# First attention of a two-layer kernel: keys on the partitions, one head with 512 queries as the unit

## The reference

```python
q = (rms_norm(x_q, q_norm_g) @ w_uq).reshape(B, S, 4, 192)      # 128 plain + 64 rotary features
kv = (rms_norm(x_kv, kv_norm_g) @ w_ukv).reshape(B, S, 4, 256)   # k_nope 128, v 128
s = (einsum('bqhd,bkhd->bhqk', qn, k_nope)
     + einsum('bqhr,bkr->bhqk', qr, k_rope)).astype(float32) * 192 ** -0.5
mask = pq[:, None, :, None] >= positions[:, None, None, :]
p = softmax(where(mask, s, neg), axis=-1)
o = einsum('bhqk,bkhd->bqhd', p, v)
y_a = o * silu(gate_a)
mix = concatenate([y_a, y_b], axis=-1) @ w_out
x = layer_norm(alpha * x + mix)
```

## Time and profile before

| | before |
|---|---|
| median of 3 runs | 3818.19 us |
| the profiled execution | 3818.23 us |
| its span | 3816.4 us |
| TensorE matmul busy | 3511.4 us (92%) |
| TensorE weight loads | 1921.9 us (50%) |
| VectorE busy | 1800.6 us (47%) |
| ScalarE busy | 1434.4 us (38%) |
| GpSimd busy | 415.0 us (11%) |
| mean DMA rate | 53 GB/s |

### The profile page before, as it was taken

The page is one execution under the profiler, slowest core; times in us unless marked ns, Lnnn a source line. Parts: engine busy times, 40 slices in busy tenths (PEclk is TensorE's granted clock), DMA queues, the critical chain, the costliest instruction groups (busy, mean ns, idle before and its releaser), DMA issues.

```text
span 3816.4 us, 38713 instructions
## 1 busy us (share of the span) xinstructions
PE 3511.4 (92%) x14032; PEld 1921.9 (50%) x14032; DVE 1800.6 (47%) x4239; ACT 1434.4 (38%) x2445; POOL 415.0 (11%) x445
## 2 busy tenths in 40 slices
PE   8999999999999999999979989899897898787887
PEld 3445644564456446645545445654445643444653
DVE  3413322332232323234662577825778616878652
ACT  1213312341233114222331465515665515766551
POOL 0001011002100210011111201202011111010100
PEclk9999999999999999989989999899998999898999
DMA  4121013002300220041103121031110031110002
GB/s 175 55 83 39 1 61 121 12 1 72 121 1 6 77 89 1 28 149 63 60 9 113 61 67 37 23 99 55 61 42 1 23 113 44 47 53 1 1 8 82
DMA packets 71885, 205.55 MB, mean 54 GB/s; under 512 B 6376, under 2 KB 7952, under 8 KB 71440
## 3 DMA queue, kind: packets, MB, share of 16 engines
q1 hardware_dynamic: 63360, 187.32, 15.3%
q10 hardware_dynamic: 8336, 15.74, 1.1%
HBM read 185.46 MB, written 17.58 MB: 53 GB/s over the span
## 4 chain that ended last, share of the span: by engine, by line
PE 73%; DVE 12%; ACT 8%; issue 5%; DMA 1%; SPq 0%; POOL 0%; ACTq 0%; DVEq 0%; POOLq 0%
PE bank L1859 37%; PE bank L1961 6%; PE o_acc L1987 6%; PE bank L1965 3%; PE bank L1977 3%; PE bank L2199 3%; PE bank L2084 3%; PE bank L2211 2%; ACT prob_t L1123 2%; PE bank L2116 2%; PE o_acc L2225 2%; ACT pt_last L1123 1%; DVE rstd L1519 1%; PE bank L2065 1%; DVE tmp L1571 1%
## 5 line engine op out<-in xcount | busy, mean ns | idle before, releaser
L1859 PE MATMUL bank<-group_even,weights 128*128 128x512 f32 x1376 | 601.5, 595 | 17.1 <-DMA weights<-in_w_in_kv 11.7
L1859 PE MATMUL bank<-group_odd,weights 128*128 128x512 f32 x1376 | 607.8, 599 | 6.2 <-ACT tmp L1109 6.2
L1859 PE MATMUL bank<-y_all,weights 128*128 128x512 f32 x1024 | 441.6, 593 | 12.9 <-DVE y_all L1426 6.0
L1859 PEld LDWEIGHTS bank<-group_even,weights 128*128 128x128 f32 x1376 | 260.7, 191 | 337.0 <-issue 336.9
L1859 PEld LDWEIGHTS bank<-group_odd,weights 128*128 128x128 f32 x1376 | 262.9, 193 | 331.6 <-issue 331.3
L1859 PEld LDWEIGHTS bank<-y_all,weights 128*128 128x128 f32 x1024 | 193.9, 190 | 255.8 <-issue 241.1
L1397 DVE CUSTOM_DVE_ANT_0 probs<-bank,mask 128x512 f32<-128x512 f32 x172 | 108.5, 687 | 261.9 <-PE bank L1965 261.9
L1961 PE MATMUL bank<-k_nope,q_nope 128*128 128x512 f32 x512 | 231.1, 594 | 0.0
L2199 PE MATMUL bank<-kh,qa 64*128 64x512 f32 (+3 forms) x816 | 175.0, 501 | 31.0 <-DVE mx L1781 18.7
L1250 ACT ACTIVATE prob_t<-bank 128x512 f32<-128x512 f32 (+3 forms) x240 | 116.7, 535 | 148.6 <-PE bank L2211 148.3
L2225 PE MATMUL o_acc<-prob_t,v 128*64 128x128 f32 x1680 | 148.7, 285 | 11.1 <-ACT prob_t L1250 7.3
(11 more groups left out here) (386 smaller groups left out, 5564.2 us busy)
## 6 DMA issues: line engine op xcount, KB each, us to landing
weights<-in_w_in SPq DMA_DIRECT2D x101, 512.0 KB, 3.5
weights<-in_w_in_q SPq DMA_DIRECT2D x64, 512.0 KB, 3.5
weights<-in_w_out SPq DMA_DIRECT2D x64, 512.0 KB, 3.6
weights<-in_w_i SPq DMA_DIRECT2D x20, 512.0 KB, 3.5
group_even<-in_x_t SPq DMA_DIRECT2D x8, 1024.0 KB, 8.0
group_odd<-in_x_t SPq DMA_DIRECT2D x8, 1024.0 KB, 8.8
group_even<-x_t SPq DMA_DIRECT2D x8, 1024.0 KB, 8.3
group_odd<-x_t SPq DMA_DIRECT2D x8, 1024.0 KB, 7.2
```

Source lines behind the costliest of these rows:

```text
L1859: ins = M(bank(*name)[:], ring[n % SLOTS][:, k * P:(k + 1) * P], rhs[:, k, :], start=(k == 0), stop=(k == chunks - 1))
```

## The change

Scores are made with the keys on the partitions and the 512 queries of the group along the free axis (the key tile is stationary, the queries move). The probabilities then have the layout that the value product needs, and `val` is the stationary operand with 512 queries moving, so nothing is turned. A step is a pair of key tiles, one with its rotary features on either half of the partitions. Per step:
- VectorE drains each score tile with `min(score, (query position - key position) * 2^80)`, which is the mask, and keeps a running maximum lane by lane over the pairs of the head (`lane_max2`).
- The head's maximum is folded, turned by TensorE (`peak`), reduced, spread by ScalarE, turned back (`spread`) and copied by ScalarE to a tile `peaks` that has each query's maximum on all partitions.
- VectorE subtracts it from the scores, two tiles in one op (`shift`), and ScalarE takes the exponential, 1024 wide. `shift` of pair n stands 9 steps behind its scores, `value` 10 steps.
- The sum over keys: GpSimd adds the tiles of 7 of the 8 pairs of heads 0 to 2 and of 4 of the last head, VectorE the rest (`total`); a matmul with ones folds the partitions (`sums`).

Twelve pairs of score tiles are held, in `probs`, `lat`, `turns`, half of the unused x buffer and a part of `y_all`. So the x of the next group is loaded after the first tile of `1out`; before, it was loaded ahead of the weights of that tile. Two of the four `gate_a` projections move from the query stage into the loop. The first `1out` tile takes its chunks in the order 4 to 7, 0 to 3 and waits for the last head only ahead of the last chunk. The bf16 mask tile goes.

```diff
+LAG = 10
+KEY_SLOTS = 12
+def key_tiles(p):
+    a, j = p // BG, p % BG
+    return [(2 * a + e) * BG + j for e in range(2)]
+def sums_by_pool(u):
+    return 7 if u < H1 - 1 else 4
 def mla_steps(g):
+    total = H1 * PAIRS_1
+    for s in range(total):
+        u, p = s // PAIRS_1, s % PAIRS_1
+        yield ("score", s)
+        if s == PAIRS_1:
+            yield from [("peak", 0), ("gate_a", 2), ("spread", 0)]
+        elif u > 0 and p == 0:
+            yield ("peak", u - 1)
+        elif u > 1 and p == 1:
+            yield ("spread", u - 1)
+        if s >= LAG:
+            yield ("value", s - LAG)
+        if s >= LAG - 1:
+            yield ("shift", s - LAG + 1)
+        if u > 1 and p in (1, 2, 3):
+            yield ({1: "total", 2: "sums", 3: "share"}[p], u - 2)
+    u = H1 - 1
+    v = total - PAIRS_1
+    yield from [("shift", v - 1), ("value", v - 2), ("peak", u), ("value", v - 1), ("spread", u), ("total", u - 1), ("gate_a", 3),
+                ("sums", u - 1), ("shift", v), ("shift", v + 1), ("value", v)]
+    for n in range(v + 1, total):
+        if n + 1 < total:
+            yield ("shift", n + 1)
+        if n == v + 2:
+            yield ("share", u - 1)
+        if n == total - 1:
+            yield from [("total", u), ("sums", u)]
+        yield ("value", n)
+    yield ("share", u)
...
     @block.sync
-                if name[0] == "1out" and name[2] == 0 and name[1] + 1 < G:
+                if name[0] == "1out" and name[2] == SLOTS and name[1] + 1 < G:
...
+                    wait_tile(sp, "1out", name[1], 0)
                     load_x(name[1] + 1, A["x_t"])
...
     @block.gpsimd
+                for kind, n in mla_steps(g):
+                    u, p = n // PAIRS_1, n % PAIRS_1
+                    if kind == "shift" and p < sums_by_pool(u):
...
+                        pool.wait_ge(probs_made, pairs_before(g, n) + 1)
...
+                            pool.wait_ge(far_sum, before)
+                            sum_of(pool, pool.tensor_tensor(sum_pool, sum_pool, tiles[:, 0, :], ALU.add))
+                            pool.tensor_tensor(sum_pool, sum_pool, tiles[:, 1, :], ALU.add).then_inc(far_sum, 1)
...
     @block.scalar
+                    elif kind == "shift":
+                        act.wait_ge(shifted, pairs_before(g, n) + 1)
+                        tiles = key_slot(g, n)
+                        A_(tiles, tiles, ACT.Exp, scale=QK_DIM ** -0.5).then_inc(probs_made, 1)
...
     @block.vector
                     if kind == "score":
...
+                        for e, t in enumerate(key_tiles(p)):
+                            wait_tile(dve, "score", g, n, e)
+                            drains(V.scalar_tensor_tensor(out=tiles[:, e, :], in0=query_pos, scalar=pos_q[:, t:t + 1],
+                                                          in1=bank("score", g, n, e)[:], op0=ALU.subtract, op1=ALU.min), "score", g, n, e)
...
+                            step(dve, V.tensor_tensor(lane_max2, lane_max2, tiles, ALU.max))
+                        if p == PAIRS_1 - 1:
+                            V.tensor_tensor(max_dve, lane_max2[:, 0, :], lane_max2[:, 1, :], ALU.max).then_inc(lane_max, 1)
...
+                    elif kind == "shift":
...
+                        V.tensor_tensor(tiles, tiles, wide(peaks[u % 2], 2), ALU.subtract).then_inc(shifted, 1)
+                    elif kind == "total":
...
+                        for p in range(first, PAIRS_1):
+                            tiles = key_slot(g, n * PAIRS_1 + p)
+                            dve.wait_ge(probs_made, pairs_before(g, n * PAIRS_1 + p) + 1)
+                            if p == first:
+                                step(dve, V.tensor_tensor(sum_dve, tiles[:, 0, :], tiles[:, 1, :], ALU.add))
+                            else:
+                                for e in range(2):
+                                    step(dve, V.tensor_tensor(sum_dve, sum_dve, tiles[:, e, :], ALU.add))
+                        dve.wait_ge(far_sum, pool_sums_before(g, n * PAIRS_1) + first)
+                        V.tensor_tensor(sum_dve, sum_dve, sum_pool, ALU.add).then_inc(lane_sum, 1)
...
     @block.tensor
                     if kind == "score":
...
+                            M(bank("score", g, n, e)[:], k_nope[:, h, t * P:(t + 1) * P], q_nope[:, h, :], start=True, stop=False)
+                        at = p * P
                         for e in range(2):
+                            half = slice(e * ROPE, (e + 1) * ROPE)
+                            M(bank("score", g, n, e)[:], k_rope[half, at:at + P], q_rope[half, h, :],
+                              start=False, stop=True).then_inc(tile_ready, 1)
...
                     elif kind == "value":
...
+                        pe.wait_ge(probs_made, pairs_before(g, n) + 1)
+                        for e, t in enumerate(key_tiles(p)):
+                            ins = M(o_acc[h % 2][:], val[:, t, h * P:(h + 1) * P], key_slot(g, n)[:, e, :],
+                                    start=(p == 0 and e == 0), stop=(p == PAIRS_1 - 1 and e == 1))
                         ins.then_inc(pv_done, 1)
+                    elif kind == "sums":
+                        pe.wait_ge(lane_sum, units_before(g, n) + 1)
...
+                            ins = M(bank("sums1", g, n)[:, b:b + 1], sum_dve[:, b * P:(b + 1) * P], ones[:, 0:1], start=True, stop=True)
...
+                    for n, k in enumerate((4, 5, 6, 7, 0, 1, 2, 3)):
+                        if c == 0 and k == H1 - 1:
+                            pe.wait_ge(y1_made, units_before(g + 1, 0))
```

More of the change, by code:

```diff
@@ L61, in first_pair_steps @@
     yield from [("v", g, b) for b in range(BG)]
-TILES_1 = S // TB
-def mla_units(g):
-    return [(BG * g + b, h) for b in range(0, BG, 2) for h in range(H1)]
-def mla_steps(g):
[L74 to L96, removed]
@@ L99, in mla_tiles @@
-def mla_tiles(g):
[L101 to L109, removed]
+PAIRS_1 = NB // 2
+LAG = 10
[3 more added lines that the diff above has]
+    return [(2 * a + e) * BG + j for e in range(2)]
@@ L112, in query_tiles @@
+def mla_tiles(g):
+    for kind, n in mla_steps(g):
+        if kind == "score":
+            yield from [("score", g, n, e) for e in range(2)]
+        elif kind in ("peak", "spread", "sums", "share", "gate_a"):
+            yield ({"share": "share1_t", "sums": "sums1"}.get(kind, kind), g, n)
 def query_tiles(g):
@@ L122, in query_tiles @@
         yield ("1var", g - 1)
-    yield from [("gate_a", g, j) for j in range(2, 4)]
     yield from [("u", g, j) for j in range(4)]
@@ L1380, in _ @@
                                                   in1=y_of(g)[:, 4 + j, :], op0=ALU.mult, op1=ALU.mult), "mix", g, j)
-                units = mla_units(g)
                 dve.wait_ge(pool_step, POOL_STEPS * (g + 1))
-                for st in mla_steps(g):
-                    kind, u = st[:2]
-                    i, h = units[u]
+                step(dve, V.tensor_scalar(query_pos, pos_k[:, g * TB:(g + 1) * TB], 0.5, FAR, ALU.add, ALU.mult))
+                for kind, n in mla_steps(g):
                     if kind == "score":
[L1388 to L1408, removed]
-                    elif kind == "sums":
[L1410 to L1422, removed]
-                                               gate[:, first:first + 2, at:at + 2 * P], ALU.mult), "share1_t", i, h // 2)
-                        wait_drained(dve, "share1_t", i, h // 2)
-                        dve.wait_ge(pv_done, (len(units) * g + u + 1) * TILES_1)
-                        V.tensor_tensor(y_of(g)[:, first:first + 2, at:at + 2 * P],
-                                        o_acc[h // 2][:].rearrange("p (h t) -> p h t", h=2), share, ALU.mult).then_inc(y1_made, 1)
@@ new lines, in _ @@
+                        for e in range(2):
+                            wait_drained(dve, "score", g, n, e)
+                        if p == 0:
+                            held_tiles = tiles
+                        elif p == 1:
+                            if units_before(g, u) > 0:
+                                before = units_before(g, u) - 1
+                                wait_tile(dve, "peak", before // H1, before % H1)
+                            step(dve, V.tensor_tensor(lane_max2, held_tiles, tiles, ALU.max))
+                        else:
+                            step(dve, V.tensor_tensor(lane_max2, lane_max2, tiles, ALU.max))
```

203 lines of the change are left out of this document (122 added, 81 removed).

## The result

The changed kernel takes 3905.27 us (median of 4 runs, 3904.05 to 3909.8) against 3818.6 for the one before: ratio 1.0229, 95% interval 1.0212 to 1.0247. It is slower, as forecast, by 86.7 us where the forecast had 64, and 0.3 us above the end of its range.

What follows compares the result with a forecast made beforehand. TensorE was taken to bound the kernel before; after the change, turns between VectorE and GpSimd were to make each loop 193.3 us against 177.3, +16 a loop and +64 in all, 3882 us. The range was 3785 to 3905, the forecast's own 3868 to 3898.

Steps and rivals of the forecast that it cites:

- TensorE's own work: Attention loops: TensorE's work falls to 159 us a loop from 175, gate projections left out.
- the turns: Attention loops: GpSimd's adds and VectorE's maximum and shift hold one another; main forecast, chance 0.57.
- the step of 5.8: Middle of a loop: add, maximum, second add, shift in turn make a step with adds 5.8 us.
- head edges: Middle of a loop: VectorE's extra work per head put at 0, at most +5 us.
- the ring: Attention loops: score, maximum, shift, exponential, value take 5.2 + 4.69 us over two steps, so 4.95 a step without turns.
- no hold: Rival: adds fall under score ops, steps 4.95 us, loop 177, kernel within 6 us of 3818; chance 0.16.
- Clock: Rival: half clock behind the two tail waits of about 5 us adds up to 20 us, 3900; chance 0.08.
- start, to score step 11: Loop start: 11 score steps, two transposes, first wait and value pair, 37.7 us without gate projections.
- middle: Score steps 11 to 31: 18 steps with adds at 5.8 us and 2 at 4.95, 114.3 us.
- tail: Loop end: 22.7 us of work plus waits, 38.4 us without gate projections.
- TensorE stays the bound: Rival: scores to probabilities under 4.69 us, steps 4.69, loop about 167 us, kernel 3778; chance 0.19.
- the lag doesn't help: Attention loops: ten steps of lag don't relieve the 4.95 us ring, as shifts queue behind their step's scores on VectorE.

Runs made afterwards that it cites:

- the better order and filled waits: Against the changed kernel: maximum behind the shift, head's maximum turned behind the value pair, shifts 24 and 25 earlier, ten unused matmuls a loop in tail waits; 3800.15 us.
- the pair of runs above: Changed kernel with GpSimd's adds cut from 512 to 16 columns, 3844.99 us; with each add replaced by three memsets, 3845.18 us.
- The run with the maximum moved: Changed kernel with each step's running maximum behind the shift on VectorE, adds left whole; 3832.84 us.
- with filled waits: In the table: changed kernel with 15 unused matmuls a loop in TensorE's long waits, order unchanged; 3889.5 us.
- the reordered one: Changed kernel with maximum behind the shift, head's maximum turned behind the value pair, shifts 24 and 25 earlier, no unused matmuls; 3806.83 us.
- thin adds: Changed kernel with GpSimd's adds over the keys cut from 512 to 16 columns, most of the softmax sum left out; 3844.99 us.

## Why the prediction was right and wrong

**Right: TensorE's own work.** Four 128-row records and four 64-row ones take 1.81 us (372.08 to 373.89) and 1.06 (to the transposes at 374.95), a value pair 1.82 (370.26 to 372.08), as worked out. The 64-row pairs still start together, as the 1.06 for four records says. Steps with scores alone are 2.97. The forecast had 159 us of TensorE work a loop. With the better order and filled waits, at a clock of 1.00, the first loop has 182.1 us busy, which is 160 without the two projections (13.7) and the ten unused matmuls (8.6, at 0.86 each).

**Right: the turns, and the step of 5.8.** The order add, maximum, add, shift is the one forecast, and steps in which it appears took 5.7 us. That 20 steps took 111.9 us against 114.3 is in part luck: fewer steps than the 18 are that long, and head edges, which the sum put at 0, have both shorter and longer ones. The score ops are free of it. Taking the GpSimd adds' reads away brought 60 us. The Trainium skill (SBUF — State Buffer, section Who interferes with whom) states that an op with two SBUF inputs contends with a GpSimd op that reads SBUF, and not with one that only writes it; the pair of runs above agrees on both halves (1.73 and 2.17 against 1.22 us with adds, 1.22 with memsets). On the price the measurement decides: a held maximum ends 1.07 us after the add (371.56 to 372.63), not 1.22.

**Right: the ring.** With no hold at all the kernel was still 26 us slower than before, where my rival *no hold* had put it within 6. Its stretch was right (102.8 us in the middle, 101.9 - 2.9 = 99 + 4 of head work forecast); what it lacked lies in the tail, 45.5 us against 41.2 (33.3 + 6.9 + 1.0): TensorE's granted clock there is 0.89 and its work takes 36.2 us against 30.6. That is the term below; filled waits weren't tried on this kernel. The run with the maximum moved shows that the ring through both VectorE ops was the place.

**Wrong: the clock.** The step that failed is the bullet *Clock*: "For the point I leave it out", with a chance of 0.08. The tail of the sum had two waits of about 5 us, and the earlier trace rows show a wait of 5.4 with 0.50 behind it. The reason given was that the waits might be shorter and would then leave the clock as it is. The waits were indeed a little shorter, 13.5 us in the first tail and not 15.7, and the clock fell all the same, behind the one of 2.6 us too. The trace of the kernel before has such a case in its second layer, a wait of 2.65 us with 1.00 ahead of it and 0.59 behind:

```profile
3301.66 1.50 PE L2133 MATMUL bank<-ident,y_all 128*128 128x128 f32 x8 [2.65 <-DVE y_all L1697]
...
3298.00:3301.66 3.66, 1.01 (x5) 1.00 0.32 128
3301.66:3304.66 3.00, 3.00 (x16) 0.59 0.00 0
```

By sections, first loop, the two gate projections included (the cuts are those of the windows above):

| | forecast | measured | with filled waits |
|---|---|---|---|
| start, to score step 11 | 46.4 | 48.6 | 46.9 |
| middle | 114.3 | 111.9 | 112.9 |
| tail | 46.3 | 52.5 | 48.4 |
| sum | 207.0 | 213.0 | 208.2 |

The tail shows the term: TensorE's work in it was forecast at 30.6 us (22.7 + 6.9 + 1.0) and took 39.0, at a mean granted clock of 0.82. Near a full clock the forecast holds to 1.2 us in this loop. The kernel came out 22.7 us later than the forecast's +64; filling the waits gave 15.8 of them back. The other 7 weren't taken apart: the piece at the lower clock that was left, what the fillers delay, and errors of the other terms all lie in them. The rival that had the clock stood at 3900, and the range was cut at 3905 though its own bound (3898 and 20 more) reached 3918; its other end, 3785, left out the 3778 of a rival with a chance of 0.19.

**The rivals.** *TensorE stays the bound* fell for this kernel, but it is what the reordered one does: 98 us for 20 steps. Its condition was stated rightly (about 0.5 us less from scores to probabilities) and it was taken by order, not by cheaper ops. Of the ring the prediction said only that the lag doesn't help; the reason in the same sentence, that the shift is queued on VectorE behind the scores of its step, already points at the edit, for the maximum stood there too.

## What to carry to other kernels

- Work that moves from the busiest engine to an idle one is paid in latency as soon as it stands in the ring that feeds the busiest one. Put each in-order queue's ops in the order of who is waiting: here one op moved behind another gave back 72 of 87 us.
- VectorE ops with two SBUF inputs and GpSimd ops that read SBUF take turns here: where both stand in the path that the busiest engine waits for, add them up as one engine's work (5.7 us a step). Off that path the same adds cost 1.3 us in 20 steps. A score op with its tensor in PSUM (733 to 748 ns) and pure writes on GpSimd (maximum and shift at 1.22 us) were free of it.
- When a forecast contains TensorE waits of some microseconds, price the matmuls behind them at the lower clock level as well, and put it in the sum, not beside it.

## What wasn't expected of the hardware

- Waits of only 2.6 and 3.2 us in the tail were already followed by 0.62 and 0.50, and 10 unused matmuls a loop, which do nothing for the result, made the kernel 6.7 us faster. Another wait of 2.6 us, and one of 3.4 in the tail with thin adds, had 1.00 behind them. Waits of about 1 us in most steps of the middle left the clock at 1.00.
- In the middle of the first loop GpSimd's first add takes 1.27 us in all 16 pairs and its second 2.13 in 11 of them: it is the one that is held by VectorE, so both engines lose by the turns.
